# One column block of the output gate projected with the values, and the gated-linear products moved down VectorE's order

## What is computed

```python
proj = h @ w_in
(ml_q, ml_k, ml_v, ml_o, ml_g, na_q, na_k, na_v,
 g_q, g_k, g_v, g_g, g_a) = jnp.split(proj, pts, axis=-1)
...
ml_out = head_rms_norm(ml_h, ml_norm_g, ML_HEADS) * jax.nn.sigmoid(ml_o)   # 6 heads, 384 columns
na_out = neighbourhood_attention(na_q, na_k, na_v, na_rpb)                 # 5 heads
gla_out = head_rms_norm(gla_h, gla_norm_g, GLA_HEADS) * jax.nn.silu(g_g)   # 5 gated-linear heads
return concatenate([ml_out, na_out, gla_out]) @ w_out
```

## Time and profile before

| What | Value |
|---|---|
| runs | 843.84 us median of 3 (843.3 to 844.0) |
| profiled execution | 842.58 us, span 840.8 us |
| TensorE busy | 830.2 us, 99% of the span |
| VectorE, ScalarE busy | 612.3 us (73%), 493.7 us (59%) |
| mean granted TensorE clock | 0.998 |
| layer 0 mixer, us from the start | `v` from 36.9, mLSTM loop to 94, neighbourhood loop to 129 |
| layer 1 mixer | `v` from 460.4, mLSTM loop to 518, neighbourhood loop to 542 |

### The profile page before, as it was taken

One profiled execution on the slowest core, in us unless ns is written; L12 is line 12 of the kernel. 1 busy time (PEld: TensorE's weight loads), 2 busy tenths in 40 slices (PEclk: granted clock), 3 DMA queues, 4 the chain that ended last, 5 costly groups with the idle time before them and its releaser, 6 DMA issues.

```text
span 840.8 us, 15177 instructions
## 1 busy us (share of the span) xinstructions
PE 830.2 (99%) x6413; PEld 773.4 (92%) x6413; DVE 612.3 (73%) x850; ACT 493.7 (59%) x693; POOL 19.4 (2%) x39
## 2 busy tenths in 40 slices
PE   8999999999999999999999999999999999999997
PEld 7999998889899999999999999888998999999996
DVE  5898977779667566556577988887776776667665
ACT  7955765577665454444568647745765654454534
POOL 5000001000000000000000000010000000000000
PEclk9999999999999999999999999999999999999999
DMA  9777654544437555565446555436516455565551
GB/s 327 239 136 224 228 183 152 200 138 164 150 104 248 200 201 182 178 205 187 151 146 237 151 172 184 179 130 233 175 68 201 149 200 201 186 215 169 182 175 51
DMA packets 112973, 151.40 MB, mean 180 GB/s; under 512 B 3785, under 2 KB 92809, under 8 KB 112905
## 3 DMA queue, kind: packets, MB, share of 16 engines
q1 hardware_dynamic: 112760, 150.16, 53.5%
q10 hardware_dynamic: 144, 0.26, 0.1%
HBM read 147.92 MB, written 1.18 MB: 177 GB/s over the span
## 4 chain that ended last, share of the span: by engine, by line
PE 96%; DVE 1%; ACT 1%; DMA 1%; issue 0%; SPq 0%; ACTq 0%
PE bank L755 26%; PE bank L756 25%; PE bank L757 25%; PE bank L837 5%; PE bank L880 3%; PE bank L964 2%; PE bank L1166 1%; PE bank L1144 1%; PE bank L902 1%; PE bank L977 1%; DMA raw<-in_w_few 1%; PE bank L821 1%; PE bank L1151 0%; PE bank L1099 0%; PE bank L1114 0%; PE bank L1012 0%
## 5 line engine op out<-in xcount | busy, mean ns | idle before, releaser
L1647 DVE TENSOR_TENSOR wlo<-raw,whi 128x2048 fp32r<-128x2048 f32 (+3 forms) x140 | 298.6, 2138 | 96.2 <-ACT whi L1256 95.2
L1256 ACT ACTIVATE whi<-raw 128x2048 fp32r<-128x2048 f32 (+3 forms) x144 | 257.2, 1789 | 49.9 <-PE bank L757 39.2
L755 PE MATMUL bank<-yhi,whi 128*128 128x256 f32 x688 | 190.6, 277 | 0.0
L756 PE MATMUL bank<-ylo,whi 128*128 128x256 f32 x688 | 190.3, 277 | 0.0
L757 PE MATMUL bank<-yhi,wlo 128*128 128x256 f32 x688 | 190.3, 277 | 0.0
L756 PEld LDWEIGHTS bank<-ylo,whi 128*128 128x128 f32 x688 | 129.4, 188 | 0.8
L755 PEld LDWEIGHTS bank<-yhi,whi 128*128 128x128 f32 x688 | 129.2, 188 | 0.9
L757 PEld LDWEIGHTS bank<-yhi,wlo 128*128 128x128 f32 x688 | 129.2, 188 | 0.0
L755 PE MATMUL bank<-whi,xhi 128*128 128x512 f32 (+2 forms) x256 | 90.2, 352 | 0.3 <-issue 0.3
L757 PE MATMUL bank<-whi,xlo 128*128 128x512 f32 (+2 forms) x256 | 88.5, 346 | 0.0
L756 PE MATMUL bank<-wlo,xhi 128*128 128x512 f32 (+2 forms) x256 | 88.4, 346 | 0.0
(11 more groups left out here) (317 smaller groups left out, 1389.1 us busy)
## 6 DMA issues: line engine op xcount, KB each, us to landing
raw<-in_w_up SPq DMA_DIRECT2D x44, 1024.0 KB, 5.0
raw<-in_w_down SPq DMA_DIRECT2D x22, 1024.0 KB, 4.8
raw<-in_w_in SPq DMA_DIRECT2D x10, 1024.0 KB, 5.0
raw<-in_w_xk SPq DMA_DIRECT2D x8, 1024.0 KB, 5.4
raw<-in_w_xv SPq DMA_DIRECT2D x8, 1024.0 KB, 4.9
raw<-in_w_out SPq DMA_DIRECT2D x8, 1024.0 KB, 5.0
raw<-in_w_xq SPq DMA_DIRECT2D x8, 1024.0 KB, 5.2
raw<-in_w_xo SPq DMA_DIRECT2D x8, 1024.0 KB, 4.9
```

Source lines behind the costliest of these rows:

```text
L755: mm(o, s_hi, m_hi, start=first, stop=False, skip_group_check=True)
L756: mm(o, s_hi, m_lo, start=False, stop=False, skip_group_check=True)
L1256: A(weight(whi, gu), raw[:, gu % RING, 0:SIZE[gu]], ACT.Copy).then_inc(hi_done, 1)
L1647: tt(weight(wlo, gu), raw[:, gu % RING, 0:SIZE[gu]], weight(whi, gu), ALU.subtract).then_inc(lo_done, 1)
```

## The change

The first 128 of the 384 output-gate columns are projected with the values: a half of `v` now has 512 columns in two DMAs, a half of `o` 256. ScalarE writes their tanh right behind the copy of the values. And `decayed` moves from behind `heads_sum` to `hh == 2` of the neighbourhood loop, behind the shares of heads 2 and 3 and ahead of the second half of `xk3` and `tails`. Both hold in both layers.

```diff
-            u.append(((l, name + half), m, 4 * "ab".index(half), 4, ((c, n),)))
+            u.append(((l, name + half), m, 4 * "ab".index(half), 4, columns))
...
-    tm("v", "w_in", C_V, ML)
+    tm_of("v", "w_in", "ab", (C_V, ML), (C_O, P))
...
-    tm("o", "w_in", C_O, ML)
+    tm("o", "w_in", C_O + P, ML - P)
...
-WIDTH = {"v": ML, "nv": NA, "gv": GV, "o": ML, "gg": GV}
+WIDTH = {"v": ML + P, "nv": NA, "gv": GV, "o": ML - P, "gg": GV}
...
-                tm_unit("v", ("v0", "v1"), ML, "n1")
+                tm_unit("v", ("v0", "v1"), WIDTH["v"], "n1")
...
-                        drain(A(eo[:, int(nm[-1]), :], b[:, 0:ML], ACT.Tanh, scale=0.5))
+                        drain(A(eo[:, int(nm[-1]), P:ML], b[:, 0:ML - P], ACT.Tanh, scale=0.5))
...
-                    drain(A(mv[:, t, :, 0:DH], bank(f"v{t}")[:, 0:ML].rearrange("p (h d) -> p h d", d=DH), ACT.Copy))
+                    A(mv[:, t, :, 0:DH], bank(f"v{t}")[:, 0:ML].rearrange("p (h d) -> p h d", d=DH), ACT.Copy)
+                    drain(A(eo[:, t, 0:P], bank(f"v{t}")[:, ML:ML + P], ACT.Tanh, scale=0.5))
...
                 heads_sum(0, MLH - 1)
-                decayed()
                 split_lo("ggb")
...
                         for g in NA_PAIRS[1]:
                             shares_of(g)
+                        decayed()
                         if l:
                             half_lo("xk3", 1)
                         tails()
```

More of the change, by code:

```diff
@@ L60, in tm, with tm_of @@
     def tm(name, m, c, n, halves="ab"):
+        tm_of(name, m, halves, (c, n))
+    def tm_of(name, m, halves, *columns):
         for half in halves:
-            u.append(((l, name + half), m, 4 * "ab".index(half), 4, ((c, n),)))
+            u.append(((l, name + half), m, 4 * "ab".index(half), 4, columns))
     fm("gq", "w_few", (0, P))
```

## The result

The changed kernel takes 846.22 us (median of 8 executions, 844.69 to 848.20) against 843.92 for the kernel before in the same comparison (843.07 to 845.05): ratio 1.0031, 95% interval 1.0018 to 1.0045. It is slower by 2.3 us. The profiled execution took 848.20 us with a span of 846.5; that of before took 842.58.

A forecast was written before the change was run, and what follows sets the result against it. TensorE, holding 96% of the chain that ended last, was taken as the bound. Widths -0.23, short waits -0.60 and layer 1's products +2.53 gave +1.7 us: 843.84 + 1.7 = 845.5 us, range 844.4 to 846.6.

The forecast's parts named there:

- The products in layer 1: `decayed` ahead of `xk3`'s second half: TensorE stands still some 2.4 us and passes `kt1` 2.53 us later.
- The products in layer 0: `decayed` ahead of `tails` fits VectorE's idle 2.60 us before head 4's scores by 0.07 us: cost 0.
- The sign named for it: In layer 0, VectorE would wait less than 0.3 us for head 4's scores, with no new TensorE wait.
- The third head's wait: TensorE's short wait for VectorE between `gk` and L964 goes: -0.30 us per layer, -0.6 in all.
- The widths: Per layer, wider `v` +2.57 us, narrower `o` -2.68: sum -0.11 us.
- The step of `o` taken from `nk`: 256-column matmuls of `o` step by 117.7 ns, as in `nk`, because both follow the products with the values.
- rival 2: Third head's wait stays, as VectorE falls back as far as TensorE: 846.1 us; chance 0.14 with the even exchange.
- the even exchange: Neighbour of rival 2: 128 columns worth as much in `v` as in `o`, waits gone: +1.9, 845.8 us.
- Leaving the old place is worth 0 to TensorE: Taking `decayed` (2.53 us of VectorE) from behind `heads_sum` gains TensorE 0, since nothing on TensorE waited there.
- the bound on the wait in layer 1: Wait at `xk3`'s second half: below 2.53 - 0.2 us, above 2.53 plus a restart, some 0.1.
- the first (`o` at 113.5 ns): Rival: `o` streams at the faster 256-column price: +1.3, 845.1 us; chance 0.18.
- the third (hidden in layer 1): Rival: moved products hidden in layer 1 too, VectorE reaching `xk3`'s second half 2.4 us sooner: -0.83, 843.0 us; chance 0.06.

The follow-up runs named there:

- the second execution of after: The changed kernel once more, unchanged, with a second profiled execution (844.86 us): 845.61 us against 843.45 for the kernel before, ratio 1.0030.
- the second execution of before: The kernel before once more, unchanged, for a second profiled execution: 843.75 us.
- the version with the gaps: Changed kernel with layer 1's gated-linear products cut in three and laid into VectorE's idle times: 843.22 us against 843.51, then 842.43 against 843.10.
- experiment 1: Change in parts, against the kernel before at 843.51 us: widths alone 845.39, move alone 846.38, changed kernel with layer 1's products at their old place 843.92.

## Why the prediction was right, and where it was not

The direction, the place and the mechanism were right; the median, 846.22, is 0.7 above the predicted 845.5. That it lies within the stated range is in part luck: it is a median over two kinds of executions, and the five with the fallen clock have one of 847.5, outside the range, the other three one of 845.43. The steps one by one:

- **The products in layer 1 (+2.53).** Right in place, in its 2.35 us at `xk3` and in its 2.52 us at `kt1`, which the second execution of after shows undisturbed.
- **The products in layer 0 (0).** Right: no wait of TensorE. The sign named for it, less than 0.3 us of VectorE's idle time left, was missed on the safe side: 0.49 us is left, since `tails` came 2.29 us later and not 2.53.
- **The third head's wait (-0.30 per layer).** Right: against the second execution of before, after's second gains 0.37 us in layer 0 and 0.33 in layer 1 from the last matmul of `gk` to the first of `o`. The wait that it removes is not always the same: in layer 0, in four profiles with the old widths, L964 starts 0.31, 0.32, 0.41 and 0.86 us behind `gk`.
- **The widths (-0.11 per layer).** Mis-sized. From the first matmul of the unit to the next instruction, `v` takes 11.00 us in place of 8.42 and `o` 5.84 in place of 8.41: the exchange is worth +0.01. The step of `o` taken from `nk` (117.7 ns) was too small by 4 ns. So the neighbour of rival 2, the even exchange, was the better term. By the formula for the isolated gap on the Trainium skill's page "TensorE: Matmul & The Clock Gate" (Back-to-back issue gap), a fixed time per column and a small constant, the exchange is even; the trace agrees in the sum, with 227.2 ns for a step of `v` against 215.8 worked out from that formula.
- **Not in the sum: steps of 118 ns** in `xk0` and `xk1` of layer 0, 0.4 us together. They stood in the profiles of after and of the version with the gaps, two of each, and in neither of before, and they take back what the third head gives there. `xk2` in layer 1 has another 0.2 us of them, which are part of the 2.52. Why the step changes stays open.
- **"Leaving the old place is worth 0 to TensorE"** was wrong once the widths are taken with it: with the new widths the old place costs 1.0 us of waits per layer (experiment 1).
- **The step that failed** is the bound on the wait in layer 1, "above 2.53 plus a restart, some 0.1". I priced a wait of 2.4 us by its own length; the clock behind it costs up to 3 us more, in over half of the executions. (The 0.1 for a restart, for which the forecast named no row, is about what the first step behind the wait shows: 0.22 us in place of 0.12.) Without the fall the executions lie 1.5 and 1.65 us over before, close to the forecast's +1.7; with it, 1.9 to 4.5. Part of that closeness is luck too: put in as measured (0.0 for the widths, -0.7 for the third head, +0.4 for the steps, +2.5 for layer 1), the terms add up to +2.2, and the 0.6 between this and the medians, of three executions each, is not explained.

Of the rivals, the first (`o` at 113.5 ns) and the third (hidden in layer 1) are refuted by the rows above; the second came true only in its neighbour, the even exchange.

## What to carry to other kernels

Before moving work on an engine off the critical path, sum the idle times that it has between the new place and the next thing that the busy engine needs, and cut the work to fit them: 2.5 us in one piece cost 2.3 us or more, in three pieces nothing that these runs can tell. Price a wait of a busy TensorE by what follows it as well as by its length, and look at the granted clock of every execution, since one profile may show the one kind or the other. Two halves of a change can lean on each other, so take them apart before judging either.

## What the runs showed of the hardware

- After a standstill of TensorE of 2.1 to 2.4 us amid dense work the granted clock fell to the 1.2 GHz level in some executions and not in others of the same code (at least 8 of 14, 2 of 6 and 4 of 11, by a mean under 0.997), for up to 7 us; with the standstill filled, in none of 11. The Trainium skill's page "TensorE: Matmul & The Clock Gate" (What's actually happening) has the gate follow how busy the engine was, and the instant of a change vary between runs of one kernel; the trace agrees, and here even whether the clock fell varied.
- TensorE stopped for 2.3 and 3.9 us behind its 4368th matmul record when 9 or 17 matmuls had been added ahead of it, for under 1 us or not at all without them. With 17 it went on at 551.55; from 549 to 551 the transfers show one packet of an instruction queue, with the end of 1 MB of weights:

```profile
q8 instruction: 1, 0.02, 2.9%
```

- That packet explains the stops well. The traces have one of 16,384 bytes there in every profile. In the twelve in which TensorE pauses behind that record, it goes on 1.3 to 1.5 us after the packet's end (1.41 us with 17 matmuls, 1.39 with 9, 1.39 in the first profile of before), wherever in the span that is; in the two in which it comes there 2 us or more after the packet's end, it does not pause. That TensorE waits for this packet is inferred from these times; no row names the packet's receiver. The Trainium skill's page "Runtime: NRT & Kernel Launch" (Instruction fetch mechanics) has an engine's instructions fetched by DMA in blocks of 16 KiB while it works, at a cost that is mostly hidden; the packet's size agrees, and here the cost was not hidden, if this is what it is.
- The same form of matmul, 128 x 256, steps by 113 or 118 ns in the same unit of the same code in two executions, so a difference of 0.6 us between single profiles need not be the change's (seven of the fourteen profiles have the slower price in the first feed-forward units of layer 0).
